# Residual kept in a DRAM table, expert results added to it by accumulating scatters, a gather depth of four, no barriers around the routing

## What is computed

```python
x = x + g1 * mix                                   # mixing sub-layer (attention and short convolution)
h = rmsnorm(x, norm2_g[l]) * (1.0 + sc2) + sh2
x = x + g2 * hier_moe(h, ...)                      # top-1 of 4 groups, then top-2 of its 4 experts
return rmsnorm(x, final_g)

def hier_moe(h, ...):                              # 16 SwiGLU experts, 1024 -> 512 -> 1024
    gates = einsum(one_hot(eid), w)                # two non-zero gates per token
    for e in range(N_EXPERTS):
        hid = silu(ht @ w_gate[e]) * (ht @ w_up[e])
        y = y + gates[:, e:e + 1] * (hid @ w_down[e])
```

## Time and profile before

| | us |
|---|---|
| runs, median of 3 (lowest to highest) | 1808.65 (1799.74 to 1810.15) |
| the profiled execution's own time | 1820.14 |
| its span, on the slowest core (core 4) | 1818.6 |
| spans of the 8 cores | 1784.3 to 1818.6 |
| PE, DVE, ACT, POOL busy | 1312.2, 774.8, 849.5, 302.2 |

### The profile page before, as it was taken

How to read it: one execution, slowest core, us unless ns; L and a number is a source line. 1 busy time by engine, 2 the same in 40 slices (tenths; PEclk the granted TensorE clock), 3 DMA queues, 4 the chain that set the end, 5 groups by cost and what they waited for, 6 DMA issues and landing times.

```text
span 1818.6 us, 41144 instructions; the slowest of 8 cores (1784.3 to 1818.6 us)
## 1 busy us (share of the span) xinstructions
PE 1312.2 (72%) x14526; PEld 874.9 (48%) x14526; DVE 774.8 (43%) x1229; ACT 849.5 (47%) x1122; POOL 302.2 (17%) x317
## 2 busy tenths in 40 slices
PE   1578998778889998999875388871177787888400
PEld 1456656556666676777654255640133333444200
DVE  4467766444323331331315466755322222333266
ACT  1235566556767878888873155541021121222022
POOL 0000000000000000000000333321412222322243
PEclk9789999999999999999996699985588999999855
DMA  8749889844556665566478733204458774220376
GB/s 229 191 105 169 155 167 177 161 67 72 96 88 95 96 96 86 97 95 97 75 146 211 212 100 117 94 30 151 150 181 299 250 280 144 100 99 31 94 240 221
DMA packets 120460, 252.88 MB, mean 139 GB/s; under 512 B 25644, under 2 KB 53020, under 8 KB 120264
## 3 DMA queue, kind: packets, MB, share of 16 engines
q0 software_dynamic: 30112, 96.50, 29.9%
q1 hardware_dynamic: 90152, 153.75, 27.4%
HBM read 400.89 MB, written 89.70 MB: 270 GB/s over the span
## 4 chain that ended last, share of the span: by engine, by line
PE 46%; issue 15%; DVE 13%; DMA 11%; ACT 9%; SPq 3%; POOL 1%; DVEq 0%; ACTq 0%; POOLq 0%
PE psd L842 9%; PE psd L1542 6%; ACT arena L819 6%; PE psd L576 6%; PE psd L601 6%; PE psd L811 6%; DMA wal<-wbf 6%; PE psd L1574 4%; PE psd L1219 3%; DMA arena<-ada_w 2%; PE psd L1180 1%; DMA arena<-w_in 1%; DVE arena L1646 1%; PE psd L658 1%; DVE arena L1200 1%
## 5 line engine op out<-in xcount | busy, mean ns | idle before, releaser
L819 ACT ACTIVATE arena<-psd,arena 128x1024 bf16<-128x1024 f32 x544 | 576.7, 1111 | 225.7 <-PE psd L813 200.6
L842 PE MATMUL psd<-arena 128*128 128x129 bf16 x4352 | 313.8, 224 | 6.7 <-DVE arena L822 3.4
L842 PEld LDWEIGHTS psd<-arena 128*128 128x128 bf16 x4352 | 281.9, 100 | 44.4 <-issue 9.8
L1542 PE MATMUL psd<-wal,arena 128*128 x752 | 200.2, 406 | 48.4 <-DMA wal<-wbf 30.1
L811 PE MATMUL psd<-arena 64*128 64x128 bf16 x2176 | 190.3, 218 | 40.3 <-ACT arena L819 31.5
L813 PE MATMUL psd<-arena 64*128 64x128 bf16 x2176 | 192.6, 220 | 0.0
L811 PEld LDWEIGHTS psd<-arena 64*128 64x128 bf16 x2176 | 124.3, 94 | 126.4 <-issue 114.0
L576 PE MATMUL psd<-arena 128*128 128x256 bf16 x1024 | 158.6, 290 | 30.6 <-ACT arena L560 10.1
L1549 ACT ACTIVATE arena<-psd 128x512 f32<-128x512 f32 x47 | 28.1, 597 | 287.3 <-PE psd L1542 259.5
L601 PE MATMUL psd<-arena 128*128 128x512 bf16 x512 | 145.9, 384 | 21.4 <-DVE arena L614 10.6
L1542 PEld LDWEIGHTS psd<-wal,arena 128*128 128x128 bf16 x752 | 76.8, 102 | 171.2 <-issue 120.8
(11 more groups left out here) (222 smaller groups left out, 1582.5 us busy)
## 6 DMA issues: line engine op xcount, KB each, us to landing
wal<-wbf SPq DMA_DIRECT2D x300, 512.0 KB
wbf<-wex POOLq DMA_DIRECT2D x96, 512.0 KB, 6.4
arena<-ada_w SPq DMA_DIRECT2D x24, 1024.0 KB
arena<-xc POOLq DMA_DIRECT2D x32, 512.0 KB, 7.1
arena<-ysc SPq DMA_DIRECT2D x16, 1024.0 KB
arena<-w_in SPq DMA_DIRECT2D x12, 1024.0 KB
arena<-xo SPq DMA_DIRECT2D x16, 520.0 KB
arena<-xr SPq DMA_DIRECT2D x16, 512.0 KB
```

The lines of the kernel that those rows point to most:

```text
L819: P.op("act", lambda e: e.activation(out=Pt[pb], in_=psd[sset][:, :], func=AF.Exp, scale=rk[:, kb:kb + 1]), r=[PSK(2 * sset), PSK(2 * sset ...
L842: ins = e.matmul(omap(m), lhsT=Pt[pb][:, c * 512 + h * 128:c * 512 + (h + 1) * 128], rhs=VA[:, kb, h, :], start=(first and m % 3 == 0), st ...
L1542: ins = e.matmul(pd[:, :], lhsT=hT[b % 2][:, fc, :], rhs=ap_, start=(fc == 0), stop=(fc == 7))
```

## The change

- The residual: each tile of it is written to a DRAM table `x2tab` in the mixing stage (16 stores of 512 KB, on SP), and `x2` keeps four tiles on chip instead of 16. Tiles 4 to 15 of the input are loaded five slots later than before, after the tile that was in the buffer is stored.
- Scatters add: the scatter of a block goes to `x2tab` with `compute_op=ALU.add`, by `gidx`; `ysc` and `sidx` are gone. All scatters write the one key `x2tab`, so each waits for the one before it to land. `ysb` has four buffers.
- Gathers run four blocks ahead, with six buffers, which are zeroed behind `rl` on POOL.
- The expert slots move to where the first stage's weights were (24 KB on). Pieces 0 to 2 of the first four experts are loaded during mixing, 3 to 5 as soon as `rl` is there. The two barriers around the routing are gone.
- The index comes first: the PE operation takes only `vals[1]` and `vals[2]` (64 matmuls), `gidx` follows in six DVE operations; the gate products move from POOL to DVE behind `gidx`, and their 96 matmuls and three DVE operations (`gates`) stand behind the gate and up projection of block 0.
- Final: 16 loads of 512 KB from `x2tab` into 16 buffers, then for each tile square, `Ln`, `Exp` on ACT, the scaling on DVE, the store. The adds on POOL and DVE and the reciprocal are gone. The barrier ahead of it stays.

```diff
-    x2 = carve(8 * K, [128, 16, 1024], F32)
+    x2 = [carve(8 * K + k_ * 4 * K, [128, 1024], F32) for k_ in range(4)]
...
+        P.op("sp", lambda e: e.dma_start(out=x2tab[i * 128:(i + 1) * 128, :], in_=x2[i % 4]), r=[("x2", i % 4)], w=[("x2t", i)],
+             dma=True)
...
-        sl_at(4 * p_ + 3, 8, lambda p_=p_: [x2_load(i) for i in (2 * p_ + 4, 2 * p_ + 5) if i < NOWN])
+        sl_at(4 * p_ + 8, 8, lambda p_=p_: [x2_load(i) for i in (2 * p_ + 4, 2 * p_ + 5) if i < NOWN])
...
+    for s_ in range(NSLOT):
+        for pt in range(3):
+            sl_at(8 + 5 * s_ + pt, 9, lambda s_=s_, pt=pt: w_first(s_, pt))
...
-    P.barrier()
...
+    for s_ in range(NSLOT):
+        for pt in range(3, NPC):
+            w_first(s_, pt, dep=["rl"])
+
+    NG, AHEAD = 6, 4
+    hg = [carve(8 * K + k_ * 2 * K, [128, 1024], BF16) for k_ in range(NG)]
+    for k_ in range(NG):
+        P.op("pool", lambda e, k_=k_: e.memset(hg[k_], 0.0), r=[("x2t", i) for i in range(12, 16)] + ["rl"], w=[("hg", k_)])
...
-    for k_ in range(3):
-        P.op("pool", lambda e, k_=k_: e.tensor_tensor(out=vals[3 + k_], in0=vals[0], in1=bc3(gsp[:, k_, :], 48), op=ALU.mult),
-             r=[("vals", 0), "gsp"], w=[("vals", 3 + k_)])
...
+    mmt2(2, (1, 2))
...
+    dv(lambda e: e.tensor_tensor(out=gidx, in0=gtmp, in1=gtmp2, op=ALU.add), w=[R, "gidx"])
+    for k_ in range(3):
+        dv(lambda e, k_=k_: e.tensor_tensor(out=vals[3 + k_], in0=vals[0], in1=bc3(gsp[:, k_, :], 48), op=ALU.mult),
+           w=[R, ("vals", 3 + k_)])
+
+    def gates():
+        mmt2(6, (3, 4, 5))
+        dv(lambda e: e.tensor_copy(out=tb[:, 3:6, :].rearrange("p v b -> p (v b)"), in_=psb[6][:, 0:144]), r=[PSK(6)])
...
-    P.barrier()
...
-        P.op("pool", lambda e: e.indirect_dma_start(out=ysc[:, :], out_offset=bass.IndirectOffsetOnAxis(ap=sidx[:, b:b + 1], axis=0),
-                                                    in_=ysb[b % 2], in_offset=None, bounds_check=bound(e, "bs", 4095), oob_is_err=False),
-             r=[("ysb", b % 2), "sidx"], w=[("ysc", b)], dma=True)
+        P.op("pool", lambda e: e.indirect_dma_start(out=x2tab[:, :], out_offset=bass.IndirectOffsetOnAxis(ap=gidx[:, b:b + 1], axis=0),
+                                                    in_=ysb[b % 4], in_offset=None, bounds_check=bound(e, "bg", 2047),
+                                                    oob_is_err=False, compute_op=ALU.add),
+             r=[("ysb", b % 4), "gidx"], w=["x2tab"], dma=True)
...
-    m_gather(0)
-    m_gather(1)
+    for b in range(AHEAD):
+        m_gather(b)
...
+        if b == 0:
+            gates()
...
+        P.op("sp", lambda e, i=i: e.dma_start(out=xf[i], in_=x2tab[i * 128:(i + 1) * 128, :]), r=["x2tab"], w=[("xf", i)], dma=True)
...
-        P.op("pool", lambda e, i=i: e.tensor_tensor(out=yk[i % 4][:, 0, :], in0=yk[i % 4][:, 0, :], in1=yk[i % 4][:, 1, :], op=ALU.add),
-             r=[("yk", i % 4)], w=[("yk", i % 4)])
-        P.op("dve", lambda e, i=i: e.tensor_tensor(out=x2[:, i, :], in0=yk[i % 4][:, 0, :], in1=x2[:, i, :], op=ALU.add),
-             r=[("yk", i % 4), ("x2", i)], w=[("x2", i)])
```

126 lines of the change are left out of this document (54 added, 72 removed).

## The result

The changed kernel takes **1749.06 us** (median of 4, 1745.80 to 1751.07), the one before, beside it on the same chip, 1809.4 us; the ratio is **0.968, 95% interval 0.964 to 0.973**. It is faster, and the forecast of 1746 us was met. Its profiled execution took 1745.80 us, with a span of 1744.2 us on core 5. Executions in which the cores of one half of the chip ran at a lower granted clock are left out of every ratio and every mean of this text.

The account below looks back on a forecast made before the run. Bounds: PE in mixing, a serial chain in routing, DMA reloads then PE in experts, DMA in the final stage. Routing -21.7, mixing 0, experts +7 and final -48 sum to -62.7: 1746 us on the median, range 1715 to 1815.

Parts of the forecast that it names:

- First barrier: Routing, behind the logits: removing the barrier closes DVE's gap from 1239.95 to 1242.73, -2.7 us.
- POOL's products beside DVE: Routing: with the gate products gone from POOL, three slowed DVE operations get faster by 2.1, 2.4 and 1.3, -5.8 us.
- Gather 0 lands faster: Routing's end: with no weights issued beside it, gather 0's data is used 5.6 us after its start, not 11.3: -5.7.
- the products' +1.8: Routing's end: gate products on DVE may hold up POOL's first gathers, 0 to 5.3 us, taken as 1.8.
- Experts, gathers -8: Experts: gathers four blocks ahead instead of two remove the 8.0 us of waits for gathers.
- Experts, adding +15: Experts: adding scatters need more DMA time beside weight reloads, between 0 and +39 us, taken as +15.
- The chain: Experts: each scatter waits for the one before; binds from a landing L of 5.9 us, just the limit, taken as 0.
- rival 1: Experts: the chain of scatters binds moderately, L of 7 to 9, +54 in place of +15, 1785 us; chance 0.24.
- Final: Final stage: moves 16.8 MB instead of 25.2 at 300 GB/s, 56 us of transfer, -48 us.
- Rival 4: Final stage: stores queued behind 16 loads leave DMA at 233 GB/s, -32, 1762 us; shares the forecast's chance of 0.52.
- 2 (L of 10.5): Experts: the chain of scatters binds hard, +136 in place of +15, 1867 us; chance 0.12.
- 3 (adding for nothing): Experts: adding costs nothing visible and weight waits shrink too, -15 and -10, 1721 us; chance 0.12.

Follow-up runs that it names:

- e4: The changed kernel with both barriers around the routing put back; 1761.92 us, ratio to before 0.977.
- e6: The changed kernel with the gate products back on POOL, ahead of the index; 1753.8 and 1756.2 us.
- e5: The changed kernel with DVE's gate products held back until gathers 0 to 2 have landed; 1745.48 us, ratio to before 0.968.
- e1: The changed kernel with scatters that write instead of add, each still waiting for the one before; 1724.80 us, ratio to before 0.955.
- e7: The changed kernel with gathers two blocks ahead instead of four; 1755.7 us, ratio to before 0.973.
- e8: The changed kernel with weight pieces 0 to 3 reloaded behind the gate and up projection, only the down projection waiting for 4 and 5; ratio to before 0.963.
- e11: e8 with scatters that write instead of add; 1706.18 us, ratio to before 0.945.
- e2: The changed kernel with scatters adding into separate rows of `ysc`, so none waits for another; 1755.15 us, ratio to before 0.972.
- e3: The changed kernel with each residual tile loaded twice in the final stage, moving 25.2 MB again; 1774.99 us, ratio to before 0.983.

## Why the prediction was right

The total was right, but part of that is luck: three misses cancel. Routing and final brought more than forecast, the experts cost more. By stage, forecast and measured as means over the cores: mixing 0 and -2.4, routing -21.7 and -26.5, experts +7 and +12.2, final -48 and -52.0; together -62.7 and -68.7. Against an ordinary execution of before, by the estimate above, the experts cost about 20 and not 12, and the sum is near the 60 of the medians. So the experts' term is off by 13 us, and routing and final make up for 9 of them.

- **First barrier, -2.7.** The gap on DVE closed by 2.7 (2.79 idle to 0.1). But the barrier also stood in the lists of ACT and PE: from the first routing operation to the block of 1536 elements (L1421, now L1429) the chain is 26.7 us instead of 28.6. Another -1.9 that the forecast, which read DVE's first gap alone, left out. e4 put 4.8 back for this barrier, near the sum of the two, though split otherwise (3.7 at DVE's gap, 0.9 in this chain, 0.4 up to the copy of the tables). The -1.9 stands in two rows of before (core 4), where DVE waits for ACT's and PE's first work behind the barrier; at these places it idles 0.45 and 0.10 us in the changed kernel:

```profile
1245.18 0.23 DVE L1360 TENSOR_TENSOR arena<-arena 128x64 f32<-128x64 f32 x1 [1.90 <-ACT arena L1367]
...
1259.67 0.69 DVE L1400 COPY arena<-psd 128x512 f32<-128x512 f32 x1 [1.41 <-PE psd L1387]
```

- **POOL's products beside DVE, -5.8.** The three rows give -2.37, -2.36 and -1.30, **-6.0**. Right, and shown by e6.
- **Fewer matmuls, -3.6.** The rest of that stretch (from L1421 to the copy of the tables 21.95 us, now 12.06) is **-3.9**. Right.
- **Shorter chain, -1.3:** 1.4. **Second barrier and zeroing, -2.9:** from the end of the index to the gather 3.0 us, now 1.0, **-2.1**. The 0.97 that are left hold POOL's own start behind DVE.
- **Gather 0 lands faster, -5.7, against the products' +1.8:** from the gather to the transposes 11.3 us on core 4, 4.4 on core 5 after, **-6.9 with the stall in it**, where the two made -3.9 (9.5 and 4.3 as means, -5.2). The step that failed is 1.1 us of issue plus 4.0 to land: the 4.0 of the earlier trace rows are counted from the start of the issue, so the 1.1 was counted twice. 4.0 and 0.5 are 4.5, and 4.4 was measured. The stall is 0.8 (e5).
- **Block 0 without a wait for weights, -3.5:** from the transposes to the projection 6.55 us, now 3.21, **-3.3** (7.6 and 3.3 as means, -4.3). Right.
- **Gate matmuls, +2:** the first scatter is 20.8 us behind the projection before and 21.7 now, **+0.9**.
- Routing in all: forecast -21.7, measured -17.9 - 9.5 + 0.9 = **-26.5**. The steps were right, their sum was 5 short: 1.9 is the barrier's share on the other engines, 2.1 is gather 0 and block 0's weights (-9.5 for -7.4), 1.1 the gate matmuls, and the rest nearly cancels.
- **Mixing, 0:** -2.4, and PE is busy 167.9 us. Between kernels with the same mixing this milestone lies from 1228.9 to 1234.2 us, so the -2.4 is not told from 0. The 14.7 MB and SP's longer queue cost nothing that shows.
- **Experts, gathers -8:** without adding (e1) the stretch is 379.6 us for 387.3, and 0.9 more for the gates is in it: **-8.6** against the profiled execution of before. That looks right and isn't shown: against the 380 us estimated for an ordinary one next to nothing is left. e7 gives the depth alone 5.5. What takes it back in the kernel without adding stays open; the chain of scatters, which e1 keeps, is a candidate (POOL waits for a scatter there 13 times up to 1490 us).
- **Experts, adding +15:** **+21**. This is the term that was surely mis-sized. Its DMA time was nearly right (67 us for 57). What failed is the step "near the middle, because weights are waited for in bursts only": 21 of 67 us came through to the end where the forecast let 15 of 57 (39 in the first part) come. In the changed kernel they come as idle time ahead of projections (39.5 us for 20.2) and as a lower granted clock (4.5 us of PE's work), which the forecast had at nothing. Late reloads are the form and not the cause: with early ones 25 come through (e8 and e11).
- **The chain, 0, at the limit L = 5.9:** the landing is 6.3 us in the median behind the reloads and 8.5 beside them (6.6 over all), and the chain still costs nothing (e2). By the forecast's own rule, L + 1.3 against 7.2, a landing of 6.3 binds, with steps of 7.6; the steps are 7.1. The rule counts the issue twice, as with gather 0: L is counted from the start of the issue, the next scatter starts 0.8 us behind the landing, and the limit is L = 6.4. So behind the reloads the chain is exactly at the limit, and the 5.9 that was forecast fell short of the 6.3 by about as much as the limit did: luck. Beside the reloads L was inside rival 1's range, 7 to 9, yet rival 1 didn't come, because blocks there were already slower than 7.2 us for their weights, and four blocks of depth took the rest. e8 shows rival 1's mechanism at 20 us as soon as the weights are early.
- **Final, -48:** **-52**. The rate was 356 GB/s in the busy stretch and 323 over the stage, above the 300 of the earlier trace rows. Rival 4 (233 GB/s) fell; ACT is done at 1727.1 us, 17 us ahead of the end, and doesn't bound.

Of the rivals, 2 (L of 10.5) and 3 (adding for nothing) are out; 1 is there but covered. The landing of an adding scatter is 2.2 us longer beside the reloads than behind them (8.5 and 6.3), that of e1's plain one 4.3 us (7.7 up to 1490 us, 3.4 from 1500 on). The Trainium skill, "DMA: Bandwidth & Descriptors", "Latency and other measured facts", has memory latency at 0.2 us on average and 2 us under high load, which would be 1.8 us more. Both measured differences are larger, and nothing here tells latency from waiting for busy engines. The Trainium skill's "DMA: Bandwidth & Descriptors", "Anatomy of one DMA", gave an estimate of 3.2 us for the scatter. The plain one takes 3.9 in the median, the adding one 6.6.

What adding brought in all: with it the experts are 21 us longer (e1), and 8.4 MB less in the final stage are 25 us (e3). With the weights early it is 25 us against 25. So adding and the bytes that it saves about break even, and the gain of this change is the routing (27 us) and the other half of the final stage (27 us); the gathers' depth gives 5.5 by e7. Whether the 27 us of the final stage could be had without an adding scatter isn't shown: the sums on POOL and DVE would stay (38.8 and 56.3 us busy in the earlier trace rows), and no run has 16 free buffers with two rows for each token.

## What to carry to other kernels

Price a term by the cover that it has now, and then ask what stands next: 21 us of adding showed as waits for weights, and when those were mended 25 came back as waits for gathers and a lower clock, so a mended wait paid 18 us here and 22 where nothing is added. Count a long wait of PE at more than its length, since the granted clock is lower behind it. Compare the profiled execution with the kernel's other runs before reading a stage from it: some 10 us of the kernel before were that one execution's. An in-order queue that holds both a dependent store and the prefetch of later blocks ties the two: count its step against the block's, and not its buffers alone: the landing, counted from the start of the issue, and 0.8 us. A final stage that is bound by DMA is paid in bytes, once all its loads can be issued at the start: reading two rows where one sum would do costs 25 us here, about what making the sum in memory costs.

## What was not expected of the hardware

- An accumulating indirect DMA costs some 2.5 times the DMA time of a plain one for the same bytes (92 against 45 engine-us per MB with a third of gathers in it), and 1.59 instead of 1.01 us of POOL for each instruction of 128 rows.
- POOL and DVE slow each other in both directions: products on POOL stretch DVE operations from 0.96 to 3.32 us, 4.42 to 6.79 and 0.19 to 1.49; DVE's bf16 products stretch POOL's issue of a gather from 1.0 to between 1.5 and 2.5 us. The Trainium skill, "SBUF — State Buffer", "Who interferes with whom", infers that a DVE operation with two tensor inputs leaves the writing of descriptors alone. The rows of the changed kernel and of e5 show that such an operation does lengthen the issue of an indirect gather, and the measurement decides; whether it holds up the writing of descriptors or POOL's reading of the index isn't shown. The price was small, 0.8 us on the path.
- A barrier that costs DVE 2.7 us costs ACT and PE their own share where they are needed next in the same chain, 1.9 us here.
- TensorE's granted clock in the experts went from 0.944 to 0.984 as waits were taken away (after, e11), and the same matmuls took 309.8 us instead of 320.0.
